# Differential attention inside a four-part encoder trunk: half-bank turnings, a wait per map at a head's first scores, and projection chunks of 24 and 12 in alternation

## What is computed

```
def diff_attention(x, w_qkv, w_o, lam_vec, subln_g, lambda_init):
    qkv = x @ w_qkv                     # 1024 x 3072, 8 heads, two maps of 64 columns each, V of 128
    ...
    def block(args):                    # a block is 128 queries
        qb, qp = args
        s = jnp.einsum('bqhcd,bkhcd->bhcqk', qb, k).astype(jnp.float32)
        dist = jnp.abs(qp[:, None] - pos[None, :])
        s = s - slopes[None, :, None, None, None] * dist[None, None, None]
        p = jax.nn.softmax(s, axis=-1)
        a = p[:, :, 0] - lam * p[:, :, 1]
        return jnp.einsum('bhqk,bkhe->bqhe', a.astype(v.dtype), v)
    ...
    o = rms_norm(o, subln_g) * (1.0 - lambda_init)
    return o.reshape(B, S, H * 2 * dh) @ w_o
```

## Time and profile before

| | |
|---|---|
| median of 3 runs | 2976.95 us (2975.7 to 2981.74) |
| profiled execution, its own time | 2978.02 us |
| span of that execution, first to last instruction | 2976.2 us |
| mean granted TensorE clock over the span | 0.974 of 2.4 GHz |
| busy share of PE, DVE, ACT, POOL over the span | 93%, 61%, 30%, 42% |
| heads 0 to 6 of this stage | about 76 us each, from 64 to 592 us |
| head 7, with no projections beside it | 592 to 678 us |

### The profile page before, as it was taken

How to read it: one execution, slowest core, us unless ns; L and a number is a source line. 1 busy time by engine, 2 the same in 40 slices (tenths; PEclk the granted TensorE clock), 3 DMA queues, 4 the chain that set the end, 5 groups by cost and what they waited for, 6 DMA issues and landing times. The chain is left out here.

```text
span 2976.2 us, 36581 instructions
## 1 busy us (share of the span) xinstructions
PE 2764.6 (93%) x13387; PEld 2302.9 (77%) x13387; DVE 1801.3 (61%) x2190; ACT 895.8 (30%) x1314; POOL 1250.8 (42%) x890
## 2 busy tenths in 40 slices
PE   7999999968899999999979999998789999999998
PEld 6788888756778888887867887787667888888886
DVE  3666766654484555555573677767467554555557
ACT  3455445542311111111133555455322111111111
POOL 2444444233563333333444555555366333333335
PEclk9999999988999999999989999999899999999999
DMA  3000002215111111111121212111601111111111
GB/s 115 26 29 28 23 26 51 56 50 185 51 36 57 49 42 49 49 42 49 50 79 45 56 47 49 41 43 22 210 26 62 43 43 50 53 44 49 44 48 71
DMA packets 212649, 163.16 MB, mean 55 GB/s; under 512 B 34939, under 2 KB 194251, under 8 KB 212555
## 3 DMA queue, kind: packets, MB, share of 16 engines
q1 hardware_dynamic: 212411, 161.38, 18.4%
q10 hardware_dynamic: 144, 0.52, 0.0%
HBM read 137.24 MB, written 24.64 MB: 54 GB/s over the span
## 5 line engine op out<-in xcount | busy, mean ns | idle before, releaser
L1129 PE MATMUL ff_ph<-XTh,WH 128*128 128x512 f32 x1408 | 550.1, 391 | 6.8 <-PEq L41 6.8
L1129 PE MATMUL ff_ph<-XTl,WH 128*128 128x512 f32 x1408 | 549.3, 390 | 0.0
L1129 PE MATMUL ff_ph<-XTh,WL 128*128 128x512 f32 x1408 | 549.2, 390 | 0.0
L1067 POOL TENSOR_SCALAR WH<-raw_weights 128x1024 fp32r<-128x1024 f32 x128 | 153.5, 1200 | 846.6 <-PE ff_ph L1129 471.9
L1277 DVE TENSOR_SCALAR ff_C<-ff_H,ff_par 128x1024 f32<-128x1024 f32 x88 | 199.3, 2265 | 430.2 <-ACT ff_H L1225 429.5
L1069 POOL TENSOR_TENSOR WL<-raw_weights,WH 128x1024 fp32r<-128x1024 f32 x128 | 340.2, 2658 | 10.7
L1129 PEld LDWEIGHTS ff_ph<-XTh,WH 128*128 128x128 f32 x1408 | 265.4, 188 | 62.7 <-issue 7.6
L1129 PEld LDWEIGHTS ff_ph<-XTh,WL 128*128 128x128 f32 x1408 | 265.3, 188 | 55.4
L1129 PEld LDWEIGHTS ff_ph<-XTl,WH 128*128 128x128 f32 x1408 | 265.4, 189 | 55.1
L1225 ACT ACTIVATE ff_H<-ff_ph,ff_par 128x1024 f32<-128x1024 f32 x88 | 98.3, 1117 | 571.0 <-PE ff_ph L1129 571.0
L1270 DVE TENSOR_TENSOR X<-ff_po,X 128x512 f32<-128x512 f32 x288 | 192.1, 686 | 103.5 <-PE ff_po L1143 103.5
(11 more groups left out here) (222 smaller groups left out, 5952.0 us busy)
## 6 DMA issues: line engine op xcount, KB each, us to landing
raw_weights<-in_ffn_w_in SPq DMA_DIRECT2D x88, 512.0 KB, 3.8
raw_weights<-in_ffn_w_out SPq DMA_DIRECT2D x44, 512.0 KB, 3.5
raw_weights<-in_attn_w_qkv SPq DMA_DIRECT2D x24, 512.0 KB
raw_weights<-in_na_w_qkv SPq DMA_DIRECT2D x24, 512.0 KB, 4.2
wo_oraw<-heads_t SPq DMA_DIRECT2D x16, 512.0 KB, 4.7
rpb_rows<-da_rows SPq DMA_DIRECT2D x2, 3840.0 KB, 26.5
na_B<-rpb_rows SPq DMA_DIRECT2D x32, 224.0 KB, 4.2
da_E<-in_x SPq DMA_DIRECT2D x8, 512.0 KB, 5.7
```

The lines of the kernel that those rows point to most:

```text
L1067: nc.gpsimd.tensor_scalar(wh[:, slot], wraw[:, raw_slot], 1.0, 1.0, ALU.mult, ALU.mult).then_inc(w_high, 1)
L1129: last = nc.tensor.matmul(out[:, at], wt[:, slot, k * P:(k + 1) * P], x[:, k, at], start=(k == 0 and n == 0), stop=(k == KT - 1 and n == 2))
```

## The change

Four edits, all in `diff_attention_stage`.

1. **Half banks.** Each turning (of a map, and of V) becomes two groups of 4 transposes, one to each bank of `tb`; each group waits only for its own half to be free and reports on its own. ACT's copy and DVE's subtraction become two instructions of 512 elements in place of one of 1024. Semaphore counts double.
2. **Wait per map.** The waits for the stacks move from ahead of step 0's scores into `score`, each map for its own.
3. **Chunks.** The projection matmuls of steps 0 to 7 are now 24, 12, 24, 12, 24, 12, 24, 12. In steps 2 and 6 the 24 are the last 12 of one projection and the first 12 of the next.
4. **Order.** In step 2 V's turning stands between these two dozens, in step 6 the turning of map 5 does. The projections that end there (1 and 4) are taken by ACT in that same step, behind its two exponentials (`TAKE_BEHIND`), and V's high part follows the take, also behind both exponentials.

```diff
-    CHUNKS = [24, 12, 12, 24, 24, 12, 12, 24]
     EARLY = 10
+    HALF = 3 * KT // 2
+    PARTS = [[(0, EARLY, 3 * KT - EARLY)], [(1, 0, HALF)], [(1, HALF, HALF), (2, 0, HALF)], [(2, HALF, HALF)],
+             [(3, 0, 3 * KT)], [(4, 0, HALF)], [(4, HALF, HALF), (5, 0, HALF)], [(5, HALF, HALF)]]
     PV_STEPS = {1: 3, 3: 0, 5: 1, 7: 2}
...
+    TAKE = {1: 0, 4: 2, 5: 3, 0: 5}
+    TAKE_BEHIND = {2: 1, 6: 4}
+    HT = QT // 2
...
             def score(h, qt):
                 n = 8 * h + qt
                 for c in range(2):
+                    if qt == 0:
+                        pe.wait_ge(kh_dup, 2 * h + c + 1)
+                        pe.wait_ge(kl_dup, 2 * h + c + 1)
+                        pe.wait_ge(stack_low, 4 * h + 2 * c + 2)
...
             def turn_map(h, qt):
                 pe.wait_ge(combined, 8 * h + qt + 1)
-                if not (isinstance(h, int) and h == 0 and qt == 0):
-                    pe.wait_ge(t_low, t_index(h, qt))
-                for k in range(QT):
-                    last = nc.tensor.transpose(tb[:, k, :], E[:, qt % 2, 0, k * P:(k + 1) * P], ident[:])
-                last.then_inc(turned, 1)
+                for part in range(2):
+                    if not (isinstance(h, int) and h == 0 and qt == 0):
+                        pe.wait_ge(t_low, 2 * t_index(h, qt) + part - 1)
+                    for k in range(part * HT, (part + 1) * HT):
+                        last = nc.tensor.transpose(tb[:, k, :], E[:, qt % 2, 0, k * P:(k + 1) * P], ident[:])
+                    last.then_inc(turned, 1)
...
             def head(h, first, last):
-                done = 0
                 for t in range(QT):
                     if t:
                         score(h, t)
...
+                    if t == 0:
+                        if not last:
+                            project(h + 1, 0, 0, EARLY)
+                        score(h, t)
+                    if not last:
+                        project(h + 1, *PARTS[t][0])
                     if t == 2:
                         turn_v(h)
...
+                    if t == 6:
+                        turn_map(h, t - 1)
+                    if not last and len(PARTS[t]) > 1:
+                        project(h + 1, *PARTS[t][1])
...
-                    if t:
+                    if t and t != 6:
                         turn_map(h, t - 1)
...
             def take_high(i, out):
-                act.wait_ge(turned, i + 1)
-                nc.scalar.activation(out, tb[:], ACT.Copy).then_inc(t_high, 1)
+                for part in range(2):
+                    at = slice(part * HT, (part + 1) * HT)
+                    act.wait_ge(turned, 2 * i + part + 1)
+                    nc.scalar.activation(out[:, at], tb[:, at], ACT.Copy).then_inc(t_high, 1)
...
                     for c in range(2):
-                        if t == 2 and c == 1:
-                            if not first:
-                                act.wait_ge(pv_done, 4 * h)
-                            take_high(9 * h + 1, Vh[:])
                         act.wait_ge(biased[c], n + 1)
...
+                    if t in TAKE_BEHIND and not last:
+                        if TAKE_BEHIND[t] == 4:
+                            act.wait_ge(turned, 2 * (9 * h + 1) + 2)
+                        take(h + 1, TAKE_BEHIND[t])
+                    if t == 2:
+                        if not first:
+                            act.wait_ge(pv_done, 4 * h)
+                        take_high(9 * h + 1, Vh[:])
...
             def take_low(i, high, out):
-                dve.wait_ge(t_high, i + 1)
-                nc.vector.tensor_tensor(out=out, in0=tb[:], in1=high.bitcast(F32), op=ALU.subtract).then_inc(t_low, 1)
+                for part in range(2):
+                    at = slice(part * HT, (part + 1) * HT)
+                    dve.wait_ge(t_high, 2 * i + part + 1)
+                    nc.vector.tensor_tensor(out=out[:, at], in0=tb[:, at], in1=high[:, at].bitcast(F32),
+                                            op=ALU.subtract).then_inc(t_low, 1)
```

More of the change, by code:

```diff
@@ L365, in turn_map @@
                 pe.wait_ge(combined, 8 * h + qt + 1)
[L366 to L370 removed]
+                for part in range(2):
[4 more added lines that the diff above has]
+                    last.then_inc(turned, 1)
             def turn_v(h):
                 pe.wait_ge(proj_out, 6 * h + 6)
[L374 to L377 removed]
+                for part in range(2):
+                    pe.wait_ge(t_low, 2 * (9 * h + 1) + part - 1)
+                    for k in range(part * HT, (part + 1) * HT):
+                        last = nc.tensor.transpose(tb[:, k, :], raw[:, 2, k * P:(k + 1) * P], ident[:])
+                    last.then_inc(turned, 1)
             def weigh(h, q):
                 i = 4 * h + q
[L382 removed]
+                pe.wait_ge(t_low, 2 * t_index(h, 2 * q + 1) + 2)
                 if not (isinstance(i, int) and i == 0):
@@ L413, in head @@
                         spread_rms(4 * h + t // 2 - 2)
-                    if t == 2:
-                        turn_v(h)
                     if t == 0:
@@ L432, in head @@
                         weigh(h, PV_STEPS[t])
-                    if t:
+                    if t and t != 6:
                         turn_map(h, t - 1)
-                    elif not first:
+                    elif t == 0 and not first:
                         turn_map(h - 1, QT - 1)
@@ L523, in head @@
                             act.wait_ge(stack_low, 4 * h + 4)
-                        if TAKE[t] == 4:
-                            act.wait_ge(turned, 9 * h + 2)
                         take(h + 1, TAKE[t])
```

24 lines of the change are left out of this document (4 added, 20 removed).

## The result

| | before | after |
|---|---|---|
| median (6 runs each, side by side) | 2977.81 us (2975.7 to 2981.74) | 2989.94 us (2986.95 to 2992.01) |
| ratio | | 1.0038, 95% interval 1.0027 to 1.0049 |
| profiled execution, its own time | 2978.02 us | 2992.01 us |
| its span, mean granted clock | 2976.2 us, 0.974 | 2990.1 us, 0.970 |

A forecast was written before the change was run, and what follows sets the result against it. PE's list nearly full (busy 93%), PE leading steps 2 to 5 and DVE step 5 to the next step 2. 21.0 - 4.9 - 1.2 + 3.4 = +18.3 us on 2978.02, less 1.07: 2995 us, range 2979 to 3005.

The forecast's parts named there:

- Step 2, -0.27: Second dozen of projection 1 ahead of V's turning: step 5's scores at 181.62 us instead of 181.89, -0.27.
- V's high part at price 0: Step 2, V's high part behind the take: DVE's slack in steps 3 to 5 covers about 1.3 us, price 0.
- Step 6, +1.91: Step 7's scores late behind projection 4's take; spread and `finish_o` delay step 7's bias by 1.91 us a head.
- The meeting, +1.04: Stacks after step 7: POOL's second key copy now meets DVE's subtraction, adding 1.04 us a head, ends 0 and 1.1.
- Half banks, +0.07 a turning on DVE: Two half subtractions cost DVE 0.07 us more per turning; four turnings on its leading stretches, +0.3 a head.
- Head 7, -4.9: Last head: halves -4.0 (-0.8 in three even steps and at two end turnings), with first scores -4.9, ends 0 and -6.
- The -0.9 of the first scores: Head 7, waits per map: of a 2.36 us wait, half the scores move ahead, -0.9 us; price 0 in other heads.
- The clock, +3.4: Wait of 2.3 us ahead of step 2's second dozen: two clock falls of 1.7 us, +3.4, ends 0 and +11.9.
- falls in every head: Rival: the clock falls in every head behind step 2's 2.3 us wait, five more falls, 3004 us; chance 0.12.
- the meeting was there: Against the rival of no meeting of POOL and DVE in the stacks: 7 x 1.04 missing, 2988 us; chance 0.20.
- take 4 was behind the exponentials: Against the rival "faster": step 6's take not delayed in effect, `spread_rms` 2.0 us sooner, 2971 us; chance 0.12.
- half of 2.04: Rival "nets out": DVE's added waiting ahead of step 7's bias is half of 2.04 us, within 2 of 2977; chance 0.14.

The follow-up runs named there:

- e6: Kernel before plus half banks and step 2 of the change (PE and ACT lists), first scores' wait as before: ratio 0.9981, -5.6 us against before.
- e2: The change with step 7's `finish_o` moved behind the two bias instructions of that step: ratio 1.0025, +7.9 us against the kernel before.
- e1: The change with steps 6 and 7 put back as before, the rest kept: ratio 0.9981, -5.1 us against the kernel before.
- e9: Kernel before plus half banks and step 6 of the change, step 2 and first scores' wait as before: ratio 1.0005, +1.5 us against before.
- e3: The change with the stacks' second key copy on ACT behind step 7's exponentials instead of on POOL: ratio 1.0012, +3.2 us against the kernel before.
- e4: Kernel before plus half banks alone, old order of chunks and all waits as they were: ratio 0.9954, -15.2 us against before.
- e7: The change with whole banks instead of half banks, all else kept: ratio 1.0064, +19.4 us against the kernel before.
- e11: Kernel before with half banks in the last head only, whole banks in the seven others: ratio 0.9961, -10.5 us against before.
- e5: Kernel before plus half banks and the first scores' wait per map, nothing else: ratio 0.9948, -15.1 us against before.

## Why the prediction was right, and where it was not

The sign, the places and the time inside the range were right. The sum of +18.3 was 6 too high, and two of its terms, step 2 and head 7, came out near the measured value although their parts did not; so far that was luck.

- **Step 2, -0.27: right in size.** Step 5's scores came 25.33 us behind the bias of step 2, before 25.75: -0.42. That is what the forecast says, -0.27 with this bias itself 0.14 later. Take 1 ended 4.20 after the bias (4.19 assumed). The wait itself was 1.02, not 2.3. PE came late to it because the clock had fallen at step 1, and where it had not fallen (e6) the wait was 1.97.
- **V's high part at price 0: right in the loop, 0.64 in head 7.** The cover that I named, DVE's slack while PE leads, exists only where projections fill PE. In the last head it is gone, and e6 shows 0.64 us. I had written the price without that cover (1.3) and did not apply it to the one head that has none.
- **Step 6, +1.91: the mechanism right, 0.3 too large.** The chain was 10.19 us from bias 6 to bias 7 and measured 9.88. Take's end to PE 0.05 (0.15 assumed), scores to spread 1.81 (1.91), spread to bias 0.97 (1.07), take's end 4.19 and the dozen 2.86 as assumed. e2 shows `finish_o` as the gate, e1 and e9 the price of 16.6 to 17.2 us with the stacks.
- **The meeting, +1.04: measured 0.86.** 7 to 0 was 15.65 against 14.78 in e3 and 14.80 in e4. Behind the rows stands the rule that I had weighed, the Trainium skill, "SBUF — State Buffer", section "SBUF: two separate sides": the port pair is a lock for a whole instruction. The trace agrees. The copy starts at 209.81, while the key's subtraction runs until 210.83, and ends 1.93 after its start, 0.91 after that subtraction; the query's subtraction ends 1.07 after the copy; `strip` ends 1.65 after the query's subtraction and the cast 0.55 after `strip`. They ran one behind the other. The key copy at 207.77, beside the bias that reads PSUM, kept its 1.04.
- **Half banks, +0.07 a turning on DVE: right, but not all.** From bias to bias steps 0, 1 and 6 grew by 0.06 (8.08 to 8.14, e4). By the Trainium skill's fixed cost for a PSUM source ("VectorE: DVE Perf Modes", the section on the TRN2 errata) it would have been 0.125 as an estimate; the measurement decides for 0.06. What I missed is on the other side: halves shorten both waits around V's turning, by 1.07 us in all. Alone they would have made heads 0.5 shorter. The change hides this gain under its step 2 (e7), so the error cost the forecast nothing; it would have made any judgement on the parts wrong.
- **Head 7, -4.9: -5.5 in the profile, but the halves were undersized.** Alone they are worth 10.5 there (e11, a median), of which I had forecast 4.0: 0.8 in each of three even steps and at the two turnings of the end. The even steps came so (7.05 became 6.25). Step 6 and the stretch from step 7's bias to the stage's end, before and then in e11:

```profile
643.99:653.80 9.81, 5.71 (x18) 4.58 (x18) 5.40 (x10) 3.41 (x5) 3.55 (x4) 0.65 0.00 1
653.80:688.18 34.38, 14.21 (x77) 12.31 (x77) 9.71 (x15) 9.35 (x14) 10.41 (x11) 0.68 0.21 73
```

```profile
642.09:649.57 7.48, 4.07 (x24) 3.20 (x22) 5.47 (x11) 3.47 (x6) 3.54 (x4) 1.00 0.00 0
649.57:679.80 30.23, 12.41 (x77) 10.52 (x77) 10.03 (x17) 9.59 (x16) 9.67 (x11) 0.75 0.23 83
```

  Of the 9.5 us between these two last heads, 2.4 are the even steps, 2.3 step 6, where the clock now stays up, and 4.2 the end, for which I had 1.6. In the end the last `spread_rms` but one comes 1.5 us sooner behind the bias (0.8 by the copies; for the rest POOL's `root` ahead of it lasts 0.70 us, where it lasted 1.67 when it began 0.17 behind a `combine` of DVE), the last turning is through 1.0 sooner, and the stretch from the weighing's first matmul to the norm products is 1.8 shorter, because the weighing runs at the full clock (mean 1.00 in place of 0.59). So I left out two things: the clock, about 4 us, and that `spread_rms` at the end waits for the same chain. Within the change the halves gave 7.3 (e7, heads 0 to 6 included). The -0.9 of the first scores does not show (e5). One profile of this head can be several us off, so that -4.9 and -5.5 lie so near is luck in part.
- **The clock, +3.4: wrong in place and in price.** I expected falls behind step 2's wait, two of them where PE leads. One came: in head 0, behind a wait of 3.54 us; there steps 2 to 5 grew by 1.18, where in the loop they lost 0.41, so it cost 1.6. In the six loop heads the fall came behind step 1's wait of 1.77 and cost next to nothing, because PE gave about 1 us back at the next wait (1.02 and less, where it is 1.97 without a fall). e2 shows it side by side: its head 2 has such a fall and lasts 77.53, heads 1, 3 and 4 have none and last 77.47 to 77.57. The rival "falls in every head" had the count and not the price. e6 shows what a fall costs where PE leads: 1.6 us.

The 18.3 can be compared with the 10.6 at the stage's end. A head of the loop (1, 3 and 4, without the falls of before) grew by 2.45 and not by 3.0, which over seven heads is 3.9 less (step 6 and the meeting). The clock is 1.8 less (one fall of the two). Head 6 is another 1.6 less: it grew by 0.84, because in it the distance from bias 5 to 6 fell from 8.27 to 7.81 and that from 7 to head 7's first bias from 12.34 to 12.12, where both grew in the loop; the forecast had taken it for a head like the others. Head 7 is 0.6 less. That leaves 10.4. Each rival fell at its own row: the meeting was there, take 4 was behind the exponentials, and DVE's new wait was 1.64 and not half of 2.04.

## What to carry to other kernels

Try the parts of a change apart before the whole is judged: here one of four gave 15 us, and two others took back 26. Before a take is moved behind other work of its engine, follow the chain from there to the instruction that heads the next engine's list; a `finish` in front of an urgent instruction passes each microsecond on. And cost the loop's last round by itself: without the projections as cover, halves of a copy were worth ten of their fifteen microseconds there.

## What was not expected of the hardware

- The clock fell behind some PE waits of 1.57 to 2.0 us in the loop and not behind others of the same length: in all six loop heads of the change behind 1.77 or 1.78, in three of six in e6 behind 1.97, in one of six in e7 behind 1.9, in two in e5 behind 1.70 and 1.68 (not behind 1.74), in two before behind 1.57. It fell in none of the heads 1 to 5 of e4 and e9, whose longest PE waits in these heads are 1.04 and 1.35.
- The same holds far behind the change: one wait of 2.45 us in neighbourhood attention was followed by a fall in six of fourteen profiles, at 2.8 us of time.
- A fall costs by where it stands: 1.6 us a head where PE leads (e6). Ahead of a wait it costs little: all six loop heads of the change have one and last 78.4, and e9, without any, has 78.05 with a step 2 that is cheaper by 0.4.
- Two engines that lock each other out for ports lengthen both rows. Of the 42.9 us that the stack instructions show as busy in the change, 6.0 are then waiting and not work (36.9 in e3).
